# One backbone step on one core: the order of the attention stage and of its weight stream changed

## The chip, the core and the metric

One NeuronCore of a Trainium2 chip runs the whole kernel in one launch. The metric is device time in microseconds (us), median of three runs. All numbers are fp32.

Five engines work side by side, each through its own instructions in order: PE (matmuls; PEld is its weight load), DVE (vector), ACT (activation functions and copies), POOL, and SP, which here does nothing but issue the large weight transfers. They meet through semaphores.

## The reference

Two groups of 128 tokens (context and latent, 256 columns together), width 1024, two layers. Cut to the stage that matters here, layer 0:

```python
h = rmsnorm(x, norm_mix_g[l]) * (1 + sc1) + sh1          # sh1, sc1, g1, sh2, sc2, g2 from silu(cond) @ w_ada[l]
a, q, k, v = split_ab(h @ w_in)                          # 512 pooling, 512 query, 128 key, 128 value columns
y = concatenate([pool_mixer(a, w_pool, pool_scale),      # centred means of 2, 4, 8, 16 tokens, then 4 matmuls
                 attention(q, k, v, sink)], axis=-1)     # 8 heads; latent queries see latent and cached keys
x = x + g1 * (y @ w_out)
h = rmsnorm(x, norm_ffn_g[l]) * (1 + sc2) + sh2
x = x + g2 * hierarchical_moe(h, ...)                    # router, then 16 experts of 3 matrices, 2 per token
```

Layer 1 has a convolution module in the place of pooling and attention, and then its own router and experts. Each layer's six modulation vectors need a 1024 by 6144 matrix `w_ada`.

## The kernel before, in words

**The weight stream.** All large weights come through SP in tiles of 2 MB (the last input tile has 1 MB), 131 of them, in one order, `STREAM`, written by `weight_stream`. `("in", 0, n)` are the three tiles of the input projection: 0 the pooling columns, 1 the queries, 2 keys and values. `("out", 0, n)` are the two of the output projection: 0 the rows that the pooling half multiplies, 1 the rows of the heads' half. `ADA_...` are groups of modulation tiles, each named after the stage in which it is read. `w1`, `w3`, `w2` are the experts' tiles, six for a pair of experts.

**Slots.** A tile lands in one of nine places: six ring slots, and `spare`, `bench` and `back`, which other data occupy until the points named in `joins`. `place_tiles` gives each tile of the stream, in order, the first free slot in the order in which slots become free. Where the slot was used, SP waits until PE has finished the tile that was there (`tiles_used`, a count that PE raises in stream order). SP's queue is strictly in order: a load that waits holds back all behind it, even those whose slot is free.

**PE's order** is the order of the code: transposes and norm, `ADA_SCALE_0` and `ADA_SHIFT_0`, the projections of pooling, queries, keys and values (`project`), two tiles of `ADA_PROJ_0`, the rotation of queries and keys, two more tiles, context and latent scores, `ADA_SOFTMAX_0`, the four tiles of `ADA_ROUTE_0`, 24 transposes of the probabilities, the pooling matmuls, probabilities times values, the output projection (pooling half, then heads), the norm, and the router (`moe`), where the two tiles of `ADA_ROOT[0]` are read. Then eight pairs of experts. `ada_rows` multiplies one modulation tile; at the end of a group ACT copies the sums (`take_part`), `ada_turn` transposes them on PE, and DVE adds the bias (`take_mod`).

**Softmax.** DVE takes one maximum for all heads and both groups, ACT makes 16 exponentials with their sums, DVE divides, PE transposes, and DVE and ACT copy the six transposed banks back in turns.

Of the kernel before, what the change touches and what calls it, by code (L numbers as in the profile page):

```python
# [15 lines left out]
P = 128  # L16
# [6 lines left out]
DC = D // P  # L23
# [80 lines left out]

def weight_stream():
# [13 lines left out]
def place_tiles():  # L119

    joins = {ADA_ROUTE_0[-1]: (BENCH, SPARE), ADA_ROOT[0][-1]: (BACK,),
# [24 lines left out]
def backbone(nc, x_prompt, x_sample, cache_k, cache_v, c, c_ctx, w_ada, b_ada, norm_mix_g, norm_ffn_g,  # L146
# [3 lines left out]
    with ExitStack() as ctx:  # L150
# [8 lines left out]
        ps_part = ps[:, 7, :]  # L159
        ps_ada = ps[:, 6, 384:480].rearrange("p (m g) -> p m g", g=2)  # L160
# [164 lines left out]
        kv_ready = sem("kv_ready")  # L325
        scores_done = sem("scores_done")
# [93 lines left out]
        def product(eng, done, kind, l, k):  # L420


            if k < DC - 2:
                eng.wait_ge(done, k // 2 + 1)
            else:
                used(eng, (kind, l, 1))
# [8 lines left out]
        LAST_IN = ("in", 0, 2)  # L435

# [78 lines left out]
        def _(pe):  # L515
# [3 lines left out]
            def ada_rows(keys, j):  # L519

                landed(pe, keys[j])
                w = wtile(keys[j])
                if j == 0 and ADA[keys[0]]:

                    pe.wait_ge(part_ready, ADA[keys[0]])
                for k in range(FC):
                    for h in range(2):
                        at = 2 * (ADA_MOST - 1 - (j - j % 2 + h))  # L530
                        last = mm(ps_part[32 * k:32 * k + 32, :], csil[:, j % 2 * FC + k, at:at + 32],
                                  w[:, k, h * TW:(h + 1) * TW], j == 0 and h == 0, True)
                last.then_inc(tiles_used, 1)
# [73 lines left out]
            def project(key, out, ready=None):  # L607
                landed(pe, key)
                w = wtile(key)
                for m in range(4):  # L610
# [4 lines left out]
                last.then_inc(tiles_used, 1)  # L615

            project(("in", 0, 0), lambda m: psx[:, m, :], h_ready)
            project(("in", 0, 1), lambda m: psx[:, 4 + m, :])
# [26 lines left out]
            for i in range(4):  # L645
                for r in range(2):
                    lo, hi = 64 * r, 64 * r + 64
                    kv = (2 * i + r) // 4
                    mm(ps[:, r, i * P:(i + 1) * P], qT[lo:hi, i, 0:TG], kT[lo:hi, int(kv != r), 0:TG])
            nc_last = None  # L650
            for i in range(4):
                for keys in range(2):
                    for r in range(2):
# [4 lines left out]
                        nc_last = mm(ps[:, 2 + 2 * r + i // 2, at:at + P], qT[lo:hi, i, TG:NT], k)  # L658
# [7 lines left out]
            for n in range(24):  # L666
                if n % 8 == 0:
                    pe.wait_ge(probs_ready, n // 8 + 1)
                last = nc.tensor.transpose(ps[:, n // 4, (n % 4) * P:(n % 4 + 1) * P], probs[:, n, :], ident)  # L669
                if n % 4 == 3:  # L670
                    last.then_inc(pt_done, 1)
            pe.wait_ge(pt_ready, 6)
            pe.wait_ge(pooled_ready, 1)
            for m in range(4):
                last = mm(psx[:, 4 + m, :], poolw[:, m, :], apad[:, m, :, APAD:APAD + TG])
            last.then_inc(pool_done, 1)
# [15 lines left out]
            ada_turn(ADA_ROUTE_0)  # L692
            for n in range(2):
                key = ("out", 0, n)
                landed(pe, key)
                w = wtile(key)
                if n == 0:
                    pe.wait_ge(pool_mixed, 1)
                for m in range(DC) if n else (4, 5, 6, 7, 0, 1, 2, 3):
                    if n == 0 and m == 0:  # L700
                        pe.wait_ge(heads_mixed, 1)
                    for k in range(FC):
                        last = mm(psx[:, m, :], w[:, k, m * P:(m + 1) * P], mixT[:, FC * n + k, :],
                                  n == 0 and k == 0 and m % 2 == 0, n == 1 and k == FC - 1)
                    if n == 1 and m in (1, 3, 5):
                        last.then_inc(y_done[0], 1)
                    if n == 1 and m == DC - 2:

                        for k in range(DC // 2):
                            norm_sum(1, k)  # L710
                last.then_inc(tiles_used, 1)
# [177 lines left out]
            def crowded(l, i):  # L889

                n = i + l * PAIRS
                with nc.body(f"pe_crowded_{n}", parent=pe_at[n], valid_engines=[mybir.EngineType.PE]):

                    pe.wait_ge(ysel_lo[0], n)
                    pe.wait_ge(ysel_hi[0], n)
                    way = pe.value_load(path[0:1, i:i + 1], min_val=0, max_val=2)
# [26 lines left out]
            def moe(l, n):  # L923

                pe.wait_ge(mod_taken, (4, 8)[l])
                for j in range(len(ADA_ROOT[l])):
                    ada_rows(ADA_ROOT[l], j)

                for k in range(DC):
                    pe.wait_ge(h_ready, DC * n + k + 1)  # L930
                    for g in range(2):
                        last = mm(ps_logit[:, g, 0:20], hT[:, k, g * TG:(g + 1) * TG],
                                  wr[:, l, k, :], k == 0, k == DC - 1)
                last.then_inc(route_done, 1)
                ada_turn(ADA_ROOT[l])

                for g in range(2):
                    for k in range(DC):
                        last = nc.tensor.transpose(ps[:, 2 * g + k // 4, (k % 4) * P:(k % 4 + 1) * P],  # L939
                                                   hT[:, k, g * TG:(g + 1) * TG], ident)  # L940
                        if k % 4 == 3:
                            last.then_inc(htok_done, 1)
                pe.wait_ge(mask_ready, l + 1)
# [4 lines left out]
                mm(ps_rank[:, 2, :], ones[:, :], mask[:, 1, :], False, True).then_inc(rank_done, 1)  # L948
                pe.wait_ge(htok_ready, 4 * l + 4)
# [3 lines left out]
                locate(l, 1, ps[:, 7, NT:NT + 1])  # L953
                gather(0, 0, 1)
                for i in range(PAIRS):
# [117 lines left out]
        def _(act):  # L1073
# [71 lines left out]
            def take_first_parts():  # L1145
# [6 lines left out]
            used(act, ("in", 0, 0))  # L1152
            act.wait_ge(s_fill, 3)
            nc.scalar.activation(apad[:, :, :, APAD:APAD + TG],
                                 psx[:, 0:4, :].rearrange("p c (g t) -> p c g t", g=2), ACT.Copy).then_inc(a_ready, 1)
# [6 lines left out]
            take_part(ADA_PROJ_0)  # L1162

            take_part(ADA_SOFTMAX_0)

            act.wait_ge(nmax_ready, 1)
            for h in range(NH):
                nc.scalar.activation(probs[:, h, :], ps[:, h // 4, (h % 4) * P:(h % 4 + 1) * P], ACT.Exp,
                                     bias=nmax[:, 0, h:h + 1], scale=SCALE,
                                     accum_out=rsum[:, 0, h:h + 1]).then_inc(exp_ready, 1)  # L1170
# [855 lines left out]
```

## Time and profile before

| what | us |
|---|---|
| median of three runs (819.95 to 824.09) | 822.08 |
| span of the profiled execution | 821.7 |
| PE busy in it | 760.8 (93%) |
| DMA: 289.67 MB moved | mean 353 GB/s |

The profile is of one execution, whose span is 0.4 below the median of the runs. Times in rows are us from the span's start. "ring<-in_w_ada" names what a row writes and reads; L517 is the line of the helper `mm`, so nearly every matmul bears it, and its tiles tell them apart: `ring,csil` are modulation tiles, `back,ring` projections, `ring,work` experts. One fp32 matmul shows as two records. "PEclk" is the granted share of TensorE's full clock.

### The profile page before, as it was taken

To read this page: it belongs to the slowest core of one execution; us is meant where nothing else is said; L and a number is where in the kernel's file an instruction comes from. 1 tells how busy PE (TensorE), PEld (TensorE's weight loads), DVE (VectorE), ACT (ScalarE), POOL (GpSimd) and SP (SyncE) were. 2 spreads that over 40 slices of the span, in tenths; PEclk is the share of its full clock that TensorE was granted. 3 is DMA by queue.
4 is the path that set the end of the run, shared out by engine and by line. 5 is a ranking of instruction groups with operands and counts; after the bars stand their busy time and mean duration, and the time that the engine had idled before them with its cause. 6 is when DMAs were issued, how large, how long until landed. Compare 5 with 4: busy or idle time off the path is not lost.

```text
span 821.7 us, 10485 instructions
## 1 busy us (share of the span) xinstructions
PE 760.8 (93%) x4071; PEld 426.7 (52%) x4071; DVE 235.0 (29%) x667; ACT 165.6 (20%) x373; POOL 50.2 (6%) x74
## 2 busy tenths in 40 slices
PE   4699889999999999999799999999998989999796
PEld 4387458754344434443488758683334353333344
DVE  2301331531111111011779931451211112121115
ACT  3210420330100010001502862451010000110012
POOL 5023000010000000000100000001000000001000
PEclk9899999889999999999999999969998999999988
DMA  9997999879999999999995259577999909999941
GB/s 293 400 398 256 412 409 430 345 284 427 424 427 426 426 429 425 426 427 413 398 399 228 108 216 429 194 298 313 430 422 424 392 18 424 428 428 427 419 172 55
DMA packets 42643, 289.67 MB, mean 353 GB/s; under 512 B 4418, under 2 KB 5902, under 8 KB 30291
## 3 DMA queue, kind: packets, MB, share of 16 engines
q1 hardware_dynamic: 36752, 275.78, 81.9%
q0 software_dynamic: 5056, 11.98, 3.9%
q10 hardware_dynamic: 770, 1.06, 0.4%
q8 instruction: 39, 0.64, 0.3%
q14 instruction: 26, 0.21, 0.1%
HBM read 285.63 MB, written 8.52 MB: 358 GB/s over the span
## 4 chain that ended last, share of the span: by engine, by line
PE 75%; DMA 16%; issue 3%; DVE 3%; ACT 1%; SPq 1%; POOL 1%; PEld 0%; DVEq 0%; PEldq 0%; POOLq 0%
PE ps L517 71%; DMA ring<-in_conv_w 4%; DMA back<-in_moe_w 4%; DMA spare<-in_moe_w 3%; DMA ring<-in_w_in_ab 3%; DMA ring<-in_w_ada 3%; DVE work L1747 1%; SPq L463 1%; PE ps L939 1%; PE ps L807 1%; PE ps L741 1%; DVE rstd L1484 0%; PE ps L778 0%; POOL work L1365 0%; PE ps L669 0%
## 5 line engine op out<-in xcount | busy, mean ns | idle before, releaser
L517 PE MATMUL ps<-ring,work 128*64 128x512 f32 x1088 | 304.5, 595 | 3.0 <-issue 2.0
L517 PEld LDWEIGHTS ps<-ring,work 128*64 128x64 f32 x1088 | 94.6, 137 | 144.9 <-issue 144.8
L517 PE MATMUL ps<-back,ring 128*128 128x256 f32 x656 | 148.3, 388 | 6.3 <-DMA ring<-in_conv_w 2.6
L517 PEld LDWEIGHTS ps<-back,ring 128*128 128x128 f32 x656 | 125.7, 194 | 28.1 <-issue 4.2
L517 PE MATMUL ps<-bench,work 128*64 128x512 f32 x208 | 96.1, 611 | 2.0 <-DVE work L1704 1.4
L517 PE MATMUL ps<-spare,work 128*64 128x512 f32 x176 | 80.4, 611 | 4.7 <-issue 4.7
L517 PE MATMUL ps<-back,work 128*64 128x512 f32 x160 | 72.0, 597 | 0.0
L1747 DVE TENSOR_TENSOR work<-work,ps 128x256 f32<-128x256 f32 x34 | 19.4, 611 | 162.9 <-PE ps L517 162.9
L517 PE MATMUL ps<-ring,csil 128*32 128x512 f32 x352 | 44.4, 633 | 8.1 <-DMA ring<-in_w_ada 8.1
L1911 DVE SCALAR_TENSOR_TENSOR work<-work,dw 128x256 f32<-128x256 f32 x120 | 50.8, 479 | 1.0
L1198 ACT ACTIVATE work<-ps 128x512 f32<-128x512 f32 x17 | 10.1, 597 | 200.8 <-PE ps L517 200.8
L517 PEld LDWEIGHTS ps<-bench,work 128*64 128x64 f32 x208 | 27.8, 140 | 29.0 <-issue 28.7
L517 PEld LDWEIGHTS ps<-spare,work 128*64 128x64 f32 x176 | 24.3, 141 | 34.3 <-issue 34.3
L517 PE MATMUL ps<-work 128*128 128x256 f32 x176 | 40.9, 386 | 0.0
L517 PEld LDWEIGHTS ps<-work 128*128 128x128 f32 x176 | 32.6, 190 | 12.9 <-issue 8.9
L1191 ACT ACTIVATE work<-ps 128x512 f32<-128x512 f32 x18 | 10.8, 597 | 121.6 <-PE ps L741 97.0
L1431 POOL DMA_INDIRECT part<-hbuf,row_at x14 | 14.4, 1026 | 298.4 <-PE ps L741 274.6
L517 PE MATMUL ps<-work,xtok 128*128 128x128 f32 x128 | 22.1, 346 | 8.2 <-issue 5.1
L517 PEld LDWEIGHTS ps<-back,work 128*64 128x64 f32 x160 | 20.8, 137 | 16.7 <-issue 16.7
L1769 DVE COPY work<-ps 128x512 f32<-128x512 f32 x11 | 7.6, 691 | 74.3 <-PE ps L517 74.3
L517 PEld LDWEIGHTS ps<-ring,csil 128*32 128x32 f32 x352 | 11.9, 113 | 32.0 <-issue 19.5
L517 PE MATMUL ps<-back,ones 128*128 128x256 f32 x96 | 24.6, 408 | 3.8 <-ACT back L1111 2.2
(238 smaller groups left out, 636.4 us busy)
## 6 DMA issues: line engine op xcount, KB each, us to landing
ring<-in_moe_w SPq DMA_DIRECT2D x63, 2048.0 KB, 19.3
ring<-in_w_ada SPq DMA_DIRECT2D x22, 2048.0 KB, 18.3
bench<-in_moe_w SPq DMA_DIRECT2D x12, 2048.0 KB, 20.5
spare<-in_moe_w SPq DMA_DIRECT2D x11, 2048.0 KB, 20.6
back<-in_moe_w SPq DMA_DIRECT2D x10, 2048.0 KB, 21.8
ring<-in_conv_w SPq DMA_DIRECT2D x6, 2048.0 KB, 24.3
ring<-in_w_in_ab SPq DMA_DIRECT2D x2, 2048.0 KB, 25.0
ring<-in_w_out_ab SPq DMA_DIRECT2D x2, 2048.0 KB, 21.2
```

The source lines that it names most:

```text
L463: sp.dma_start(dst, src.rearrange("(k p) n -> p k n", p=P)).then_inc(slot_full[SLOT[n]], 16)
L517: return nc.tensor.matmul(out, lhsT, rhs, start=start, stop=stop, skip_group_check=True)
L741: last = nc.tensor.transpose(ps[:, 4 + half, (k % 4) * P:(k % 4 + 1) * P], hrows[:, k * P:(k + 1) * P], ident)
L807: last = nc.tensor.transpose(ps[:, 6 + f // 2, (f % 2) * P:(f % 2 + 1) * P], hid[:, f * P:(f + 1) * P], ident)
L939: last = nc.tensor.transpose(ps[:, 2 * g + k // 4, (k % 4) * P:(k % 4 + 1) * P], hT[:, k, g * TG:(g + 1) * TG], ident)
L1191: nc.scalar.activation(hsel[:, 0:4, :], ps[:, 4, :].rearrange("p (k j) -> p k j", k=4), ACT.Copy).then_inc(hsel_lo[which], 1)
L1198: nc.scalar.activation(sil, ps[:, 6, :], ACT.Silu).then_inc(sil_ready[r], 1)
L1431: nc.gpsimd.indirect_dma_start(hrows, None, hbuf[l], IndirectOffsetOnAxis(ap=row_at[:, 0:1], axis=0), bounds_check=NT - 1, oob_is_err=Fals ...
L1747: V.tensor_tensor(hid[:, h * 2 * P:(h + 1) * 2 * P].rearrange("s (f p) -> s f p", f=2), sil.rearrange("s (p f) -> s f p", f=FC)[:, f, :], ...
L1769: V.tensor_copy(ysel[:, 512:1024], ps[:, 5, :]).then_inc(ysel_hi[r], 1)
L1911: V.scalar_tensor_tensor(out=cv[k], in0=upad[:, k, :, t:t + TG], scalar=dw[:, k, t:t + 1], in1=cv[k], op0=ALU.mult, op1=ALU.add).then_inc( ...
```

## The change

The same work is done; its order changes.

- **Stream.** Queries, then keys and values, come first; the pooling tile follows two tiles of `ADA_PROJ_0`. The output tiles come before `ADA_ROUTE_0`, the heads' half first.
- **PE.** Half of the pooling projection stands between the rotation and the latent scores, half after them; then the context scores. Probabilities are transposed in two parts, with modulation work between. The heads' half of the output projection comes first, with the pooling matmuls (now in other PSUM banks) in its middle. The four tiles of `ADA_ROUTE_0` move into the router, one of them in two halves between the router's own matmuls; `ADA_ROOT[0]` moves behind the ranks.
- **ACT and DVE.** Maxima, exponentials and divisions are made for the latent group first, then for the context group. DVE takes over the copy of the pooling columns.
- **Waits.** POOL's first gather of layer 0 waits for the turned `ADA_ROOT[0]`; rounds with a crowded expert wait for the gathered rows.

```diff
-    return (ADA_SCALE_0 + ADA_SHIFT_0 + [("in", 0, n) for n in range(3)] + ADA_PROJ_0 + ADA_SOFTMAX_0
-            + ADA_ROUTE_0 + [("out", 0, n) for n in range(2)] + ADA_ROOT[0] + moe(0)
+    return (ADA_SCALE_0 + ADA_SHIFT_0 + [QUERY_IN, LAST_IN] + ADA_PROJ_0[0:2] + [POOL_IN] + ADA_PROJ_0[2:4]
+            + ADA_SOFTMAX_0 + [HEADS_OUT, POOL_OUT] + ADA_ROUTE_0 + ADA_ROOT[0] + moe(0)
...
-    joins = {ADA_ROUTE_0[-1]: (BENCH, SPARE), ADA_ROOT[0][-1]: (BACK,),
+    joins = {HEADS_OUT: (BENCH, SPARE), ADA_ROOT[0][-1]: (BACK,),
...
-            fit = [f for f in free if expert or f[0] < BENCH]
+            fit = [f for f in free if expert or f[0] < SPARE or f[0] == SPARE and f[1] is not None]
...
-            ada_rows(ADA_PROJ_0, 2)
-            ada_rows(ADA_PROJ_0, 3)
-            ada_turn(ADA_PROJ_0)
-
-            pe.wait_ge(a_ready, 1)
+            landed(pe, POOL_IN)
+            project(POOL_IN, lambda m: psx[:, m, :], range(0, 2))
...
-            nc_last.then_inc(scores_done, 1)
-
-            pe.wait_ge(mod_taken, 3)
-            ada(ADA_SOFTMAX_0)
-            for j in range(len(ADA_ROUTE_0)):
-                ada_rows(ADA_ROUTE_0, j)
...
+            last.then_inc(latent_done, 1)
+            project(POOL_IN, lambda m: psx[:, m, :], range(2, 4))
+            ada_rows(ADA_PROJ_0, 2)
+
+            pe.wait_ge(a_ready, 1)
+            for i in range(4):
...
+            last.then_inc(scores_done, 1)
+            ada_rows(ADA_PROJ_0, 3)
...
+            turn_probs((2, 3, 4, 5), {2: 1, 3: 1, 4: 2, 5: 2})
+            ada_turn(ADA_PROJ_0)
+            ada_rows(ADA_SOFTMAX_0, 0)
+            turn_probs((0, 1), {0: 3, 1: 3})
+            ada_rows(ADA_SOFTMAX_0, 1)
             pe.wait_ge(pt_ready, 6)
...
+            landed(pe, HEADS_OUT)
+            pe.wait_ge(heads_mixed, 1)
+            for m in range(DC):
+                last = output(HEADS_OUT, m, True, False)
+                if m == 3:
+
+                    pe.wait_ge(pooled_ready, 1)
+                    for g in range(4):
+                        mixed = mm(ps_pool[:, g, :], poolw[:, g, :], apad[:, g, :, APAD:APAD + TG])
+                    mixed.then_inc(pool_done, 1)
+            last.then_inc(tiles_used, 1)
+            landed(pe, POOL_OUT)
+            pe.wait_ge(pool_mixed, 1)
+            for m in range(DC):
+                last = output(POOL_OUT, m, False, True)
...
+                if l == 0:
+                    for j in range(len(ADA_ROOT[l])):
+                        ada_rows(ADA_ROOT[l], j)
                 pe.wait_ge(htok_ready, 4 * l + 4)
```

What `place_tiles` makes of it, positions 13 to 27 of the stream (slots 0 to 5 are the ring; "after X" is the tile that PE must have finished first):

| position | before | now |
|---|---|---|
| 13 | `ADA_ROUTE_0[0]`, slot 1 | `HEADS_OUT`, slot 1, after `ADA_PROJ_0[1]` |
| 14 | `ADA_ROUTE_0[1]`, slot 2 | `POOL_OUT`, slot 2, after `POOL_IN` |
| 15 to 18 | `ADA_ROUTE_0[2:4]`, `("out",0,0)`, `("out",0,1)` | `ADA_ROUTE_0` |
| 19 | `ADA_ROOT[0][0]`, slot 1, after `ADA_ROUTE_0[0]` | the same tile, slot 1, after `HEADS_OUT` |
| 20 | `ADA_ROOT[0][1]`, slot 2, after `ADA_ROUTE_0[1]` | the same tile, slot 2, after `POOL_OUT` |
| 21 | first `w1`, slot 3, after `ADA_ROUTE_0[2]` | first `w1`, `bench` |
| 22, 23 | `bench`, `spare` | `spare`, slot 3 after `ADA_ROUTE_0[0]` |
| 25, 26 | after `("out",0,0)`, `("out",0,1)` | after `ADA_ROUTE_0[2]`, `[3]` |

SP's queue before, from the second group of modulation tiles to the first experts (in_w_in_ab are input tiles, in_w_out_ab output tiles, in_moe_w experts):

```order
L463 DMA ring<-in_w_in_ab 128x8x512 x2
L463 DMA ring<-in_w_in_ab 128x8x256 [waits tiles_used]
L463 DMA ring<-in_w_ada 128x4x1024 [waits tiles_used] x10
L463 DMA ring<-in_w_out_ab 128x4x1024 [waits tiles_used] x2
L463 DMA ring<-in_w_ada 128x4x1024 [waits tiles_used] x2
L480 DMA ring<-in_moe_w 128x4096 [waits tiles_used]
L480 DMA bench<-in_moe_w 128x4096 [waits s_out,pv_done]
L480 DMA spare<-in_moe_w 128x4096 [waits pool_done]
L480 DMA ring<-in_moe_w 128x4096 [waits tiles_used] x4
```

The same stretch of SP's queue now:

```order
L467 DMA ring<-in_w_in_ab 128x8x512
L467 DMA ring<-in_w_in_ab 128x8x256
L467 DMA ring<-in_w_ada 128x4x1024 [waits tiles_used] x2
L467 DMA ring<-in_w_in_ab 128x8x512 [waits tiles_used]
L467 DMA ring<-in_w_ada 128x4x1024 [waits tiles_used] x4
L467 DMA ring<-in_w_out_ab 128x4x1024 [waits tiles_used] x2
L467 DMA ring<-in_w_ada 128x4x1024 [waits tiles_used] x6
L484 DMA bench<-in_moe_w 128x4096 [waits s_out,pv_done]
L484 DMA spare<-in_moe_w 128x4096 [waits pool_done]
L484 DMA ring<-in_moe_w 128x4096 [waits tiles_used] x5
```

Four modulation tiles moved from ahead of the output tiles to behind them, so that the two tiles of `ADA_ROOT[0]`, last of the six, and behind them all expert tiles, now wait for PE to be done with the output tiles.

PE before, from the rotation to the output projection (bench,cst is the rotation, bench alone the scores, cst,work the transposes, spare the pooling matmuls, work,bench probabilities times values, cst,part a turn):

```order
L517 MATMUL ps<-bench,cst 128x512
L517 MATMUL ps<-bench,cst 128x128
L517 MATMUL ps<-ring,csil 32x512 x16
L517 MATMUL ps<-cst,part 128x4x2 x4
L517 MATMUL ps<-bench 128x128 x24
L517 MATMUL ps<-ring,csil 32x512 x16
L517 MATMUL ps<-cst,part 128x2x2 x4
L517 MATMUL ps<-ring,csil 32x512 x32
L669 MATMUL ps<-cst,work 128x128 x24
L517 MATMUL ps<-spare 128x256 x4
L517 MATMUL ps<-work,bench 64x128 x24
```

PE now, from behind the rotation to the values:

```order
L521 MATMUL ps<-back,ring 128x256 x16
L521 MATMUL ps<-bench 128x128 x16
L521 MATMUL ps<-back,ring 128x256 x16
L521 MATMUL ps<-ring,csil 32x512 x8
L521 MATMUL ps<-bench 128x128 x8
L521 MATMUL ps<-ring,csil 32x512 x8
L678 MATMUL ps<-cst,work 128x128 x16
L521 MATMUL ps<-cst,part 128x4x2 x4
L521 MATMUL ps<-ring,csil 32x512 x8
L678 MATMUL ps<-cst,work 128x128 x8
L521 MATMUL ps<-ring,csil 32x512 x8
L521 MATMUL ps<-work,bench 64x128 x24
```

The pooling projection (back,ring) now surrounds the latent scores, and the 32 matmuls of the four `ADA_ROUTE_0` tiles are gone from ahead of the transposes.

## Rows read from the trace of the kernel before

**Rows 1.** The page's second part: DMA busy tenths in 40 slices.
```profile
DMA  9997999879999999999995259577999909999941
```

**Rows 2.** By stretch: us, busy of five engines, PEclk, DMA share, GB/s.
```profile
185.00:410.00 225.00, 218.44 (x1044) 93.73 (x1040) 46.43 (x116) 28.16 (x59) 8.62 (x16) 1.00 1.01 423
```

**Rows 3.** PE's timeline: start, us, what, [idle before, releaser].
```profile
410.21 4.20 PE L517 MATMUL ps<-back,ring 128*128 128x256 f32 x12 [2.59 <-DMA ring<-in_conv_w]
```

**Rows 4.** Two transfers of line 480: start, and us to landing.
```profile
L480 SPq DMA_DIRECT2D spare<-in_moe_w x1: 328/328/328, 190.4 to 190.4; - x1
...
DMA to landing us min/median/max: 12.0/12.0/12.0
...
L480 SPq DMA_DIRECT2D spare<-in_moe_w x1: 327/327/327, 354.2 to 354.2; - x1
...
DMA to landing us min/median/max: 28.6/28.6/28.6
```

**Rows 5.** The chain of work that ended last: start, us, what; two pairs of experts.
```profile
191.74 14.25 PE ps L517 x64
...
219.04 14.25 PE ps L517 x64
```

**Rows 6.** The same chain in the attention stage.
```profile
39.62 38.20 PE ps L517 x176
...
77.93 8.55 PE ps L517 x68
...
114.54 35.22 PE ps L517 x200
```

**Rows 7.** PE's timeline in the attention stage.
```profile
87.15 1.06 PE L517 MATMUL ps<-cst,part 128*128 128x8 f32 x8 [0.73 <-ACT part L1143]
...
88.14 2.95 PE L517 MATMUL ps<-bench 64*128 64x128 f32 x48
...
91.02 3.68 PE L517 MATMUL ps<-ring,csil 128*32 128x512 f32 x32
...
110.89 2.97 PE L669 MATMUL ps<-cst,work 128*128 128x128 f32 x24
...
119.24 1.06 PE L517 MATMUL ps<-cst,part 128*128 128x8 f32 x8
```

**Rows 8.** DVE's and ACT's timeline in the softmax.
```profile
91.14 1.22 DVE L1561 TENSOR_REDUCE smax<-ps 128x8 f32<-128x1024 f32 x1 [2.70 <-PE ps L517]
...
96.68 0.37 ACT L1168 ACTIVATE work<-ps,nmax 128x128 f32<-128x128 f32 x1
...
99.44 0.51 ACT L1172 ACTIVATE work<-ps,nmax 128x256 f32<-128x256 f32 x1
...
103.03 0.31 ACT L1178 ACTIVATE esink<-esink 128x16 f32<-128x16 f32 x1
...
105.44 2.18 DVE L1577 TENSOR_SCALAR work<-work,rden 128x256 f32<-128x256 f32 x8
...
111.00 0.60 ACT L1143 ACTIVATE part<-ps 128x512 f32<-128x512 f32 x1 [7.67 <-PE ps L517]
...
119.35 1.02 ACT L1184 ACTIVATE back<-ps 128x1024 f32<-128x1024 f32 x1 [4.86 <-PE ps L517]
```

**Rows 9.** A transfer of line 463 that found the queue empty.
```profile
L463 SPq DMA_DIRECT2D ring<-in_w_ada x1: 368/368/368, 69.2 to 69.2; - x1
...
DMA to landing us min/median/max: 7.8/7.8/7.8
```

**Rows 10.** DMA issues: what, count, KB each, median us to landing.
```profile
hbuf<-xtok POOLq DMA_DIRECT2D x4, 512.0 KB, 7.5
```

**Rows 11.** As Rows 2: three stretches around waits of PE.
```profile
410.00:415.00 5.00, 4.79 (x14) 3.91 (x15) 0.14 (x1) 0.00 (x0) 0.00 (x0) 0.66 1.06 390
...
780.00:785.00 5.00, 3.52 (x10) 1.20 (x12) 0.00 (x0) 0.00 (x0) 0.00 (x0) 0.52 1.02 428
745.00:750.00 5.00, 4.03 (x20) 1.38 (x18) 0.00 (x0) 0.60 (x1) 0.00 (x0) 1.00 1.00 421
```

More of the change, by code:

```diff
@@ L418, in used, with product @@
             eng.wait_ge(tiles_used, TILE[key] + 1)
-        def product(eng, done, kind, l, k):
+        def product(eng, done, last, k):
             if k < DC - 2:
@@ L523, in ada_rows, with ada_half @@
                 landed(pe, keys[j])
-                w = wtile(keys[j])
                 if j == 0 and ADA[keys[0]]:
                     pe.wait_ge(part_ready, ADA[keys[0]])
-                for k in range(FC):
[L529 to L533, printed above, removed]
+                ada_half(keys, j, 0)
+                ada_half(keys, j, 1)
+            def ada_half(keys, j, h):
+                w = wtile(keys[j])
+                at = 2 * (ADA_MOST - 1 - (j - j % 2 + h))
+                for k in range(FC):
+                    last = mm(ps_part[32 * k:32 * k + 32, :], csil[:, j % 2 * FC + k, at:at + 32],
+                              w[:, k, h * TW:(h + 1) * TW], j == 0 and h == 0, True)
+                if h:
+                    last.then_inc(tiles_used, 1)
             def ada_turn(keys):
@@ L604, in _, with project @@
             ada(ADA_SHIFT_0)
-            def project(key, out, ready=None):
-                landed(pe, key)
+            def project(key, out, blocks, ready=None):
                 w = wtile(key)
-                for m in range(4):
+                for m in blocks:
                     for k in range(DC):
@@ L691, in _, with output @@
             last.then_inc(pv_done, 1)
[L692 to L695, printed above, removed]
+            pe.wait_ge(mod_taken, 3)
+            ada_turn(ADA_SOFTMAX_0)
+            def output(key, m, first, last_tile):
                 w = wtile(key)
[L697 to L711, printed above, removed]
+                rows = FC * (key == HEADS_OUT)
+                for k in range(FC):
+                    last = mm(psx[:, m, :], w[:, k, m * P:(m + 1) * P], mixT[:, rows + k, :],
+                              first and k == 0 and m % 2 == 0, last_tile and k == FC - 1)
+                return last
+            landed(pe, HEADS_OUT)
[7 more added lines that the diff above has]
+                    mixed.then_inc(pool_done, 1)
+            last.then_inc(tiles_used, 1)
+            landed(pe, POOL_OUT)
+            pe.wait_ge(pool_mixed, 1)
+            for m in range(DC):
+                last = output(POOL_OUT, m, False, True)
+                if m in (1, 3, 5):
+                    last.then_inc(y_done[0], 1)
+                if m == DC - 2:
+                    for k in range(DC // 2):
+                        norm_sum(1, k)
+            last.then_inc(tiles_used, 1)
             norm_sums(1, DC // 2)
@@ L925, in moe @@
                 pe.wait_ge(mod_taken, (4, 8)[l])
-                for j in range(len(ADA_ROOT[l])):
-                    ada_rows(ADA_ROOT[l], j)
+                if l == 0:
+                    ada_rows(ADA_ROUTE_0, 0)
+                    ada_rows(ADA_ROUTE_0, 1)
+                    landed(pe, ADA_ROUTE_0[2])
+                else:
+                    for j in range(len(ADA_ROOT[l])):
+                        ada_rows(ADA_ROOT[l], j)
                 for k in range(DC):
@@ L933, in moe @@
                                   wr[:, l, k, :], k == 0, k == DC - 1)
+                    if l == 0 and k in (2, 4):
+                        ada_half(ADA_ROUTE_0, 2, k // 4)
                 last.then_inc(route_done, 1)
-                ada_turn(ADA_ROOT[l])
+                if l == 0:
+                    ada_rows(ADA_ROUTE_0, 3)
+                else:
+                    ada_turn(ADA_ROOT[l])
                 for g in range(2):
@@ L948, in moe @@
                 mm(ps_rank[:, 2, :], ones[:, :], mask[:, 1, :], False, True).then_inc(rank_done, 1)
+                if l == 0:
+                    for j in range(len(ADA_ROOT[l])):
+                        ada_rows(ADA_ROOT[l], j)
                 pe.wait_ge(htok_ready, 4 * l + 4)
@@ L1185, in _ @@
             norm_act(1, (0, 24))
-            take_part(ADA_ROOT[0])
+            take_part(ADA_ROUTE_0)
             def take_low(which, count):
@@ new lines, in divisor, with divide_latent @@
+            def divisor(g):
+                dve.wait_ge(exp_ready, (NH + 1) * (2 - g))
+                link(V.tensor_tensor(rden[:, g, :], rsum[:, g, :], esink[:, g, :], ALU.add))
+                link(V.reciprocal(rden[:, g, :], rden[:, g, :]))
+            def divide_latent(first):
+                for h in range(first, first + NH // 2):
+                    last = V.tensor_scalar(probs[:, 8 + 2 * h:10 + 2 * h, :], probs[:, 8 + 2 * h:10 + 2 * h, :],
+                                           rden[:, 1, h:h + 1], None, ALU.mult)
+                last.then_inc(probs_ready, 1)
@@ L1573, in _ @@
+            divisor(1)
+            divide_latent(0)
+            dve.wait_ge(scores_done, 1)
+            bound(0, ps[:, 0:2, :], 4)
+            divide_latent(NH // 2)
+            take_turned(2, 1)
+            take_turned(4, 3)
+            divisor(0)
             for h in range(NH):
```

128 lines of the change are left out of this document (66 added, 62 removed).

## The prediction, made before the changed kernel ran

> **What bounds the kernel now.** The page gives PE 93% of the span, so I looked for the stretches in which something else sets the time. First the slices of the DMA engines [rows 1], 20.5 us each: full from the tenth to the twenty-first, 185 to 431 us, and with gaps before, in the fourth (61 to 82), the eighth and the ninth (144 to 185). Then the busy time by stretch [rows 2]: from 185 to 410 the DMA engines are never idle (share 1.01 at 423 GB/s), while PE is busy 218 of 225 us. Then PE's own waits: at 410.2, at the start of layer 1's convolution, it has waited 2.59 us for a convolution tile [rows 3]. So two things end nearly together at 410, PE's work and the weight stream, and the stream is 2.6 us later.
>
> The stream's pace and PE's differ. Position 32 of the stream is issued at 190.4 and lands 12.0 later, at 202.4; position 68, the last expert tile of layer 0, is issued at 354.2 and lands 28.6 later, at 382.8 [rows 4]. The 36 tiles between take 180.4 us, 5.01 each, which is 30.1 for the six tiles of a pair of experts, gathers included. PE needs 219.04 - 191.74 = 27.3 for a pair [rows 5]. PE can therefore live on a lead for a while, but the layer ends when the stream does. After 410 I take the rest as rigid: a shift of the convolution's start shifts the end by as much, since from there PE's chain is followed to the next stretch in which the stream waits for slots that PE sets free.
>
> The question is thus not how early PE leaves the attention stage, but when the stream starts to run without gaps. Before, that is about 185.
>
> **PE in the attention stage.** Per step, what PE has to do from 39.6 to the end of the output projection: projections 38.3 (from 39.62 to 77.93); four tiles of ADA_PROJ_0 with the rotation 8.55 [rows 6]; the turn 1.06, scores 2.95, two tiles of ADA_SOFTMAX_0 3.68, transposes 2.97 [rows 7]; the second turn about 1.06, as the first; then 35.22 for the pooling matmuls, values and output projection [rows 6], less the turn of ADA_ROUTE_0, which goes away from here (119.24 to 120.15, 0.9): 34.3. The sum is 92.9, so PE could be done at 132.5. The four tiles of ADA_ROUTE_0 (two cost 3.68 [rows 7], so 7.4) and the waits for their transfers go from here.
>
> What waits come in their place? I follow PE through the new order with the same rows. Queries and keys end at 63.4, two modulation tiles and the rotation at 68.3, half of the pooling projection (7.2 of its 14.5) at 75.6, latent scores at 77.5, the other half at 84.7, a modulation tile at 86.6, context scores at 87.5, another tile at 89.4. DVE's copy of the pooling columns is hidden: they are ready at 84.7, the maximum over as many columns costs 1.22 [rows 8], PE needs the banks at 86.6; without that cover it would cost those 1.2. The latent exponentials begin after 80 and are eight of 0.45, done before 85. Three waits stay:
> - The second half of the latent division. DVE takes four divisions (half of 2.18), the context maximum (1.22 and about 0.4 for its small steps), then four more [rows 8]: ready at 90.6, PE there at 90.4: 0.3.
> - The turn of ADA_PROJ_0. On ACT the copy of its sums now stands behind the context exponentials: maximum ready at 89.2, eight exponentials in 2.76 (96.68 to 99.44), the sink 0.31, the copy 0.60 [rows 8], so 93.0; PE has done 16 transposes and stands since 91.6: 1.4.
> - The copy of the heads' output, 1.02 on ACT [rows 8], less the turn of ADA_SOFTMAX_0 that PE does meanwhile: 0.3.
>
> That is 2.0, and the output projection ends at 134.5, against 149.8 before: 15.3 earlier. The pooling chain on POOL, the pooling matmuls and the probabilities' last copies are done before PE asks for them.
>
> **The router.** It gets 7.4 us of tiles and a turn, partly in waits that were there. Even if all 8.4 came on top, PE would reach the experts 6.9 earlier than before. That is not where the end is set.
>
> **The stream.** SP issues in order. Position 14 now waits for the pooling tile (84.7), position 19 for the heads' half of the output projection (about 118.7), position 20 for its end (134.5); the experts' tiles stand behind, those for bench and spare too, though these are free by 113. Before, positions 13 to 20 needed modulation and input tiles alone, which PE had done by 104, and the stream ran without a gap from 82 to 144.
>
> A modulation tile that found the queue empty landed 7.8 after its issue [rows 9]. So position 20 lands at 134.5 + 7.8 = 142.3, and from there nothing holds the stream: positions 23 to 27 need the tiles of ADA_ROUTE_0 and ADA_ROOT[0] done, which PE has by about 156, before the stream comes to them. Twelve tiles at 5.01 are 60.1. The two stores of the token rows (hbuf, 512 KB each [rows 10]), which fell into a gap before, now share the engines: at 423 GB/s [rows 2] 2.5 us; bounds are 0, if they fall beside other gaps, and twice as much; I take 2.5. Position 32 lands at 142.3 + 60.1 + 2.5 = 204.9, against 202.4: the stream is 2.5 us later, and stays so, since it is full from there to 410 either way. PE, 7 or more earlier, uses up its lead against the slower stream in three pairs (2.8 a pair) and then waits for tiles. The last pair's w2 waited for its tile before too, so the end of the layer moves with the stream.
>
> The sum: 821.7 + 2.5 = 824.2 for a profiled execution. The median of the runs stood 0.4 above the profiled one, so 824.5. Bounds from the unknowns: no new waits of PE (-2.0) and hidden stores (-2.5) give 820.0; a later end of the output projection counts one for one.
>
> The landing time is where the notes differ. The Trainium skill, "DMA: Bandwidth & Descriptors", section "Anatomy of one DMA", puts a transfer at 2.0 us and its bytes at 436 GB/s (fitted on GpSimd's path, while these are SP's), an estimate of 6.8 for a 2 MB tile; the row has 7.8. By the page the sum would be 823.5; I keep the row.
>
> **Rivals.**
> *The new chain through ACT and DVE is longer than its rows (slower).* ACT now holds 16 exponentials, two sinks and the copy of ADA_PROJ_0 in one line, DVE three divisions, two maxima and the pooling copy. If each step of it costs its semaphore hops and the context group comes 4 us later, PE stands at the turn of ADA_PROJ_0, the output projection ends at 138.5, and the end is 828.5. It decides from an end later than 136. For it: five hand-overs between DVE and ACT that are one now. Against it: the rows already hold such hops, and PE has modulation tiles to put between.
>
> *The clock (slower).* Starved pairs wait 2.8 us, mostly in one place, between w1 and w3. After the wait of 2.59 at 410 the granted clock was 0.66 over five us; around the longer wait of 780 it was 0.52, the lower of the two levels (1.2 of 2.4 GHz); around a wait of under 1 us at 746 it was 1.00 [rows 11]. If every starved pair falls to the lower level for some 5 us, it loses about 2.5, nearly the 2.8 it had; what is left over at the last pair, at most 2.5, is half covered by the 2.59 that PE waits at 410: end 825 to 827, say 826.5. The Trainium skill, "TensorE: Matmul & The Clock Gate", section "HAM oscillation", tells of a kernel that waits for DMA before each group of matmuls and starts each of them cold; by that rule all five starved pairs would fall.
>
> *PE sets the end after all (faster).* If the stream has slack that I don't see, for example because the gaps before cost it more than those now, PE's lead counts. The convolution could start at 410.2 - 2.6 - 6.9 = 400.7, and the end be 812.5. For it: PE's share, and no wait of PE from 185 to 380. Against it: the DMA share of 1.01 over the whole stretch.
>
> **How the numbers follow.** The forecast has 0.60, the longer chain 0.17, the clock 0.13, PE's lead 0.10. A difference under 0.5% (4.1 us) can't be told from none with runs that spread from 819.95 to 824.09. The forecast itself, 820 to 828, is 0.52 within that bound and 0.08 above; the chain is 0.14 above and 0.03 within; the clock 0.05 and 0.08; PE's lead 0.09 below and 0.01 within. Together: faster 0.09, same 0.64, slower 0.27. The range, 819.5 to 830, leaves out PE's lead and the worst of the chain; the forecast's own is 820 to 828.
>
> **What would show it.** Right: the output projection ends at 133 to 137; between 83 and 143 the DMA engines have three gaps, the last two about ten us each; from 143 to the convolution they are full; from the fourth pair on PE waits for experts' tiles; the convolution starts near 413. Wrong: gaps that are missing because the loads don't wait as I read them, a convolution that starts before 408 (then the stream was not the bound), or an attention stage that ends after 137.

## The result, and the profile of the changed kernel

| | before | changed |
|---|---|---|
| median of 4 runs each, us | 821.02 (818.44 to 824.09) | 837.77 (836.36 to 837.92) |
| ratio, with its 95% interval | | 1.0192 (1.0169 to 1.0215) |
| profiled execution, us; its span | 822.08; 821.7 | 836.36; 834.6 |

The changed kernel is 1.9% slower. The forecast was 824.5, with 819.5 to 830 as its range: wrong in size, and the time lies outside it. The page's DMA slices first, 20.9 us each here, against [rows 1]:

```profile
DMA  9999753999999999999998159577999908999951
```

The engines are full from the eighth slice to the twenty-first, and the gaps before now stand in the fifth to seventh, 83 to 146. Busy time by stretch shows the last two (columns as in [rows 2]), then the saturated stretch:

```profile
117.00:130.00 13.00, 13.00 (x62) 11.42 (x62) 1.66 (x4) 0.00 (x0) 0.00 (x0) 1.00 0.11 21
135.00:146.00 11.00, 10.71 (x49) 8.71 (x47) 3.38 (x12) 2.50 (x6) 0.00 (x0) 1.00 0.13 23
185.00:423.00 238.00, 225.10 (x1061) 98.57 (x1058) 44.08 (x110) 28.14 (x60) 8.94 (x17) 0.99 1.01 423
```

SP's transfers of positions 20, 32 and 68, which answer to [rows 4, 9]:

```profile
L467 SPq DMA_DIRECT2D ring<-in_w_ada x1: 368/368/368, 143.8 to 143.8; - x1
...
DMA to landing us min/median/max: 8.0/8.0/8.0
...
L484 SPq DMA_DIRECT2D ring<-in_moe_w x1: 328/328/328, 196.2 to 196.2; - x1
...
DMA to landing us min/median/max: 19.5/19.5/19.5
...
L484 SPq DMA_DIRECT2D ring<-in_moe_w x1: 328/328/328, 364.8 to 364.8; - x1
...
DMA to landing us min/median/max: 32.6/32.6/32.6
```

Position 20 is issued at 143.8, when the output projection's last tile has been used, and lands at 151.8. Position 32 lands at 196.2 + 19.5 = 215.7, against 202.4 [rows 4], and position 68 at 397.4, against 382.8. The stream is 13 to 15 late, and the span grew by 12.9.

So the gate works as forecast, but this last gate, the issue of position 20, opens at 143.8 instead of 134.5. Where the 9.3 went is in the chain of work that ended last, in the attention stage (start, us, what; to be held against [rows 6]):

```profile
65.46 20.86 PE ps L521 x132
86.32 0.02 issue
86.34 1.23 DVE spare L1636
...
87.91 5.17 DVE work L1622 x4
93.09 1.14 DVE smax L1606
...
95.68 2.61 DVE work L1622 x4
...
98.34 1.97 PE ps L678 x8
```

L1622 is the division of the latent probabilities. In [rows 8] eight of them took 2.18; here the first four take 5.17 and the next four 2.68 (2.61 in the chain). The same line by itself (ns of one, shortest/median/longest), and POOL's timeline at that time:

```profile
L1622 DVE TENSOR_SCALAR work<-work,rden x8: 340/878/1983, 87.9 to 97.4; 128x256 f32<-128x256 f32 x8
```
```profile
87.66 2.09 POOL L1442 TENSOR_TENSOR spare<-spare 128x1144 f32<-128x1144 f32 x1 [75.51 <-DVE spare L1636]
89.83 0.64 POOL L1447 TENSOR_TENSOR mean<-spare,cst 128x256 f32<-128x256 f32 x1
90.54 0.72 POOL L1450 TENSOR_TENSOR spare<-mean,spare 128x256 f32<-128x256 f32 x1
91.34 1.60 POOL L1442 TENSOR_TENSOR spare<-spare 128x846 f32<-128x846 f32 x1
```

The longest division, 1.98, lies beside POOL's longest sum, 2.09. The first four take 1.98, 0.79, 0.88 and 1.75, and each of them ends 0.1 to 0.2 after one of these four instructions of POOL (2.09, 0.64, 0.72 and 1.60): each of these divisions waits out one whole instruction of POOL. The pooling columns now come so late that POOL's chain runs from 87.7 to 99.7, beside DVE's divisions. PE stands behind them, and what follows the second wait is slow as well (PE's timeline, then the stretch with its granted clock, 0.56 of full):

```profile
93.14 1.09 PE L678 MATMUL ps<-cst,work 128*128 128x128 f32 x8 [2.04 <-DVE work L1622]
98.34 1.97 PE L678 MATMUL ps<-cst,work 128*128 128x128 f32 x8 [4.10 <-DVE work L1622]
100.10 1.72 PE L521 MATMUL ps<-cst,part 128*128 128x8 f32 x8
101.74 3.64 PE L521 MATMUL ps<-ring,csil 128*32 128x512 f32 x16
105.32 1.26 PE L678 MATMUL ps<-cst,work 128*128 128x128 f32 x8
```
```profile
97.00:107.00 10.00, 8.66 (x48) 5.19 (x52) 5.29 (x16) 2.67 (x9) 2.51 (x4) 0.56 0.73 272
```

The theory to be tested: DVE's divisions are slowed by POOL's pooling chain; the clock adds a part of its own; and the end follows the moment at which the output projection's tiles are free, since the experts' tiles stand behind two loads that wait for them. Rivals: something else slows the divisions, or PE's own late start at the experts sets the end.

### The profile page after: what moved, and what is told of

It reads as the page before. It is cut to its first block, busy times and chain, and to the rows that moved or that the text cites. A ratio compares the mean times of both kernels' runs of the same rounds, so it can differ in the third digit from the quotient of the medians.

```text
span 834.6 us, 10496 instructions
## 1 busy us (share of the span) xinstructions
PE 766.7 (92%) x4071; PEld 426.7 (51%) x4071; DVE 243.6 (29%) x673; ACT 164.5 (20%) x373; POOL 50.4 (6%) x74
## 3 DMA queue, kind: packets, MB, share of 16 engines
q10 hardware_dynamic: 770, 1.06, 0.4%
## 4 chain that ended last, share of the span: by engine, by line
PE 71%; DMA 17%; DVE 4%; issue 4%; ACT 1%; POOL 1%; PEld 1%; DVEq 0%; SPq 0%; PEldq 0%; POOLq 0%
PE ps L521 68%; DMA back<-in_moe_w 8%; DMA ring<-in_moe_w 4%; DMA hbuf<-xtok 2%; DMA ring<-in_w_ada 2%; DMA part<-hbuf,row_at 1%; DVE work L1813 1%; DVE work L1622 1%; PE ps L831 1%; PE ps L975 1%; DVE rstd L1530 1%; PEld ps L521 1%; PE ps L765 1%; PE ps L678 0%; POOL work L1409 0%
## 5 line engine op out<-in xcount | busy, mean ns | idle before, releaser
L521 PE MATMUL ps<-ring,work 128*64 128x512 f32 x1088 | 321.6, 598 | 12.4 <-issue 11.7
L521 PEld LDWEIGHTS ps<-ring,work 128*64 128x64 f32 x1088 | 100.6, 137 | 160.2 <-issue 160.0
L521 PE MATMUL ps<-back,ring 128*128 128x256 f32 x592 | 134.5, 387 | 3.5 <-ACT back L1177 3.1
L521 PEld LDWEIGHTS ps<-back,ring 128*128 128x128 f32 x592 | 113.5, 194 | 22.5 <-issue 5.7
L521 PE MATMUL ps<-bench,work 128*64 128x512 f32 x208 | 97.9, 620 | 3.5 <-DVEq L1526 2.0
L521 PE MATMUL ps<-ring,csil 128*32 128x512 f32 x368 | 52.0, 701 | 2.9 <-DMA ring<-in_w_ada 2.9
L521 PEld LDWEIGHTS ps<-work 128*128 128x128 f32 x176 | 32.5, 190 | 12.9 <-issue 8.9
L521 PE MATMUL ps<-back,ones 128*128 128x256 f32 x96 | 22.9, 386 | 3.8 <-ACT back L1156 2.2
```

Of the source, the lines that this page charges most:

```text
L521: return nc.tensor.matmul(out, lhsT, rhs, start=start, stop=stop, skip_group_check=True)
```

## The experiments

**The pooling chain later.** On POOL, in the changed kernel:

```diff
             pool.wait_ge(a_ready, 1)
+            pool.wait_ge(probs_ready, 3)
             src, at = apad, 0
```

> The changed kernel, with one more wait: POOL starts the pooling chain only when DVE has finished all divisions of the probabilities. Theory (DVE's divisions run slowly because POOL's pooling chain runs at the same time): the eight divisions of 128x256 take 0.27 us each, as before the change, instead of 1.29 and 0.67; PE's two waits for them, 2.04 and 4.10, shrink to about 0.3 and 1.4, the clock does not fall to 0.50 behind them; the output projection ends near 136 instead of 143.8, and the time falls by 7 to 8, to about 830. Rival A (the divisions are slow because of ACT, the PE or the transfers, not POOL): they stay at 5.17 and 2.68 for four, and the time stays at 837.8. Rival B (the end of the output projection is not what sets the time): the divisions are fast, the stage ends near 136, and the time stays above 834.

Measured: 829.09 (827.59 to 830.50, 6 runs) against 822.02 (22 runs); ratio 1.0088 (1.0057 to 1.0119). DVE's timeline, then PE's:

```profile
89.26 1.14 DVE L1623 TENSOR_SCALAR work<-work,rden 128x256 f32<-128x256 f32 x4
...
92.40 1.14 DVE L1623 TENSOR_SCALAR work<-work,rden 128x256 f32<-128x256 f32 x4
```
```profile
92.39 2.30 PE L678 MATMUL ps<-cst,work 128*128 128x128 f32 x16
95.86 1.06 PE L521 MATMUL ps<-cst,part 128*128 128x8 f32 x8 [1.18 <-ACT part L1188]
96.85 3.14 PE L521 MATMUL ps<-ring,csil 128*32 128x512 f32 x16
99.92 1.51 PE L678 MATMUL ps<-cst,work 128*128 128x128 f32 x8
```

The divisions are as fast as before, PE's two waits are gone, and the wait of 1.4 that the prediction had put at the turn appears there, with 1.18. Position 20 is issued at 138.6. That is 2.6 later than expected. Half of it is the start: this execution came to the modulation tiles and the rotation at 66.7, the changed kernel at 65.4. The other half is the clock, which I had expected to stay up (0.74 granted from 95 to 100): behind the wait of 1.18 the next tile took 3.14 instead of 1.92 and the transposes behind it 1.51 instead of 1.09. Both rivals fall: half of the loss is gone by a wait on POOL alone.

**The same collision, made in the kernel before.** There the pooling chain ran before the scores:

```diff
             pool.wait_ge(a_ready, 1)
+            pool.wait_ge(exp_ready, 17)
             src, at = apad, 0
```

> The kernel before, with one more wait: POOL starts the pooling chain only when ACT has finished the exponentials, so that it runs beside DVE's divisions (in the kernel before it ran at 56 to 69, when DVE was idle). Theory (POOL's chain slows DVE's divisions): the eight divisions of 128x256 take 5 to 10 us together instead of 2.18, and the eight of 128x128 more than 1.66 too. Rival (something else in the new order slows them): 2.18 and 1.66 as they were. The time is expected within 3 of the kernel before in either case, since there the stream does not wait for this stage; it is not the question of this run.

Measured: 828.91 in one run, span 827.1. DVE's timeline in the kernel before and here, then POOL's here:

```profile
103.86 1.66 DVE L1574 TENSOR_SCALAR work<-work,rden 128x128 f32<-128x128 f32 x8
```
```profile
104.91 5.36 DVE L1575 TENSOR_SCALAR work<-work,rden 128x128 f32<-128x128 f32 x8
110.19 6.75 DVE L1578 TENSOR_SCALAR work<-work,rden 128x256 f32<-128x256 f32 x8
```
```profile
104.54 2.09 POOL L1399 TENSOR_TENSOR spare<-spare 128x1144 f32<-128x1144 f32 x1 [92.40 <-ACT esink L1178]
```

6.75 instead of 2.18 [rows 8], and 5.36 instead of 1.66 for the eight of the context group, without any other part of the change: the cause is POOL. My expectation for the time missed. The span rose by 5.4, since in the kernel before a stream tile waits for the output projection as well: position 26, issued at 149.8 before and here at 156.2 (1.0 of it a later start of the stage), and position 32 lands 6.5 later, at 208.9.

**Two experts' tiles ahead of the two that wait.** SP alone, in the changed kernel:

```diff
-            for key in STREAM[:TILE["w1", 0, 0]]:
+            for key in STREAM[:TILE[ADA_ROOT[0][0]]]:
                 load(key)
...
                         expert_tile(i, t, 2 * i + t % 2)
+                        if l == 0 and i == 0 and t == 1:
+                            for key in ADA_ROOT[0]:
+                                load(key)
```

> The changed kernel, with one edit on SP alone: the first two experts' tiles, whose places are free when the heads' values and the pooling matmuls are done, are issued ahead of the two tiles of ADA_ROOT[0], which wait for the output projection's two tiles. PE's order is the same. Theory (the stream behind those two waits sets the time): the two experts' tiles are issued near 111 and 121 and fill the idle time of the DMA engines; the output projection still ends near 143.8; position 32 of the stream lands 10 earlier, near 206; the convolution starts near 413, and the time falls by about 10, to 828. Rival (PE's own late start at the experts, 178.1 instead of 175.0, sets the time): the tiles come earlier, PE does not, and the time stays above 834.

Measured: 826.33 (823.66 to 829.85, 11 runs) against 822.02; ratio 1.0055 (1.0033 to 1.0078). SP's timeline, then the stretch that had a DMA share of 0.11:

```profile
110.18 0.34 SPq L484 DMA_DIRECT2D bench<-in_moe_w  x1
120.26 0.34 SPq L484 DMA_DIRECT2D spare<-in_moe_w  x1
```
```profile
117.00:130.00 13.00, 13.00 (x62) 11.42 (x62) 1.66 (x4) 0.00 (x0) 0.00 (x0) 1.00 0.86 323
```

The divisions are as slow as in the changed kernel and the last gate opens at 142.7, but position 32 lands at 193.6 + 11.6 = 205.2, ten earlier, and the time falls by 11. PE begins the experts at 176.8, only 1.3 earlier. It is the stream that sets the end, and PE's start does not.

**Both edits.** The wait on POOL and the order on SP, as above.

> Both edits: the late pooling chain, and the two experts' tiles ahead of ADA_ROOT[0]. Theory: the two gains are of different kinds and add up as far as the stream goes, 7.5 + 10: position 32 near 198, experts on PE from about 171; then PE and the stream are again nearly level, and the time is 820 to 822, level with the kernel before. Rival (behind the faster stage PE's own work or the late gather of the second pair sets the time): 825 or more, with PE never waiting for a tile of the stream between 200 and 400.

Measured: 821.34 (818.17 to 824.19, 12 runs) against 822.02; ratio 0.9991 (0.9969 to 1.0014). Alone the two edits gained 8.7 and 11.4, together they gain 16.4 of these 20. Position 32 lands at 200.3 (198 was expected), and PE and the stream are nearly level, as in [rows 3]. The wait at the turn is as long as with the first edit alone, but here the clock stayed up: the tile behind it takes 1.92, not 3.14 (PE's timeline):

```profile
94.81 1.06 PE L524 MATMUL ps<-cst,part 128*128 128x8 f32 x8 [1.17 <-ACT part L1191]
95.80 1.92 PE L524 MATMUL ps<-ring,csil 128*32 128x512 f32 x16
...
408.14 3.72 PE L524 MATMUL ps<-back,ring 128*128 128x256 f32 x16 [1.98 <-DMA ring<-in_conv_w]
```

**The latent divisions on ACT.** POOL stays beside them:

```diff
+            act.wait_ge(rden_ready, 1)
+            for h in range(NH):
+                last = nc.scalar.activation(probs[:, 8 + 2 * h:10 + 2 * h, :], probs[:, 8 + 2 * h:10 + 2 * h, :],
+                                            ACT.Copy, scale=rden[:, 1, h:h + 1])
+                if h % 4 == 3:
+                    last.then_inc(probs_ready, 1)
...
-            divide_latent(0)
+            dve.sem_inc(rden_ready, 1)
...
-            divide_latent(NH // 2)
```

> The changed kernel, with the eight divisions of the latent probabilities on ACT in place of DVE; POOL's pooling chain stays where it is, beside them. Theory (only DVE is slowed by POOL): ACT's divisions take about 0.4 each whatever POOL does, 1.6 for four, and PE's two waits of 2.04 and 4.10 go; DVE's eight context divisions of 128x128 now fall beside the end of POOL's chain and take 3 to 5 instead of 1.66, which costs PE a new wait of 1 to 3 ahead of the last eight transposes. Output projection near 138.5, time near 832. Rival (whatever works on the probabilities beside POOL is slowed): ACT's divisions take over 0.8 each, and the time stays above 836.

Measured: 830.59 (828.61 to 835.89, 4 runs) against 822.77 (17 runs); ratio 1.0117 (1.0076 to 1.0157). ACT's timeline, then DVE's:

```profile
86.39 3.30 ACT L1216 ACTIVATE work<-work,rden 128x256 f32<-128x256 f32 x8 [2.13 <-DVEq L1646]
```
```profile
87.72 1.22 DVE L1613 TENSOR_REDUCE smax<-ps 128x8 f32<-128x1024 f32 x1 [1.42 <-PE ps L522]
...
89.96 1.45 DVE L1618 TENSOR_TENSOR esink<-nmax,sink 128x8 f32<-128x8 f32 x1
...
94.39 3.39 DVE L1653 TENSOR_SCALAR work<-work,rden 128x128 f32<-128x128 f32 x8
```

Beside POOL, ACT takes 3.30 for eight; in the next run, with POOL idle then, it takes 3.30 too. DVE's maximum, which reads PSUM, keeps its 1.22 [rows 8], while an addition of 128x8 out of SBUF takes 1.45, and the context divisions 3.39 instead of 1.66. So it is DVE's work on SBUF that POOL holds up; ACT, on the same probabilities, is not held up. The new wait of PE ahead of the last transposes did not come: the clock was at 0.50 from 95 to 100, and PE was late itself.

**All three edits.** The wait on POOL, the order on SP, the divisions on ACT.

> Three edits: the late pooling chain, the two experts' tiles ahead of ADA_ROOT[0], and the latent divisions on ACT. With the first two alone the run took 821.3 against 822.0 before. Theory: DVE's 2.2 of divisions leave the chain to the context maximum, PE's last wait of 1.17 in the transposes goes, the output projection ends at 134 to 135 instead of 135.9, and the time is 819 to 821. Rival (PE's waits were gone already, and ACT's divisions delay its context exponentials by 3): output projection at 137 to 138, time 822 to 824.

Measured: 819.00 (814.77 to 822.60, 12 runs) against 822.77; ratio 0.9960 (0.9939 to 0.9981). This version beats both kernels, by 0.4% the one before. But the theory missed. PE's last wait did not go, it grew from 1.17 to 1.67 (below), and from the start of the rotation's step to the last gate it took 72.0, against 70.2 with two edits. The last gate opened at 135.3 instead of 135.9 only because this execution came to that step at 63.3 instead of 65.7. The medians, 2.3 apart, come from two series of runs, and their intervals against the kernel before overlap. That the third edit adds something is therefore not shown, and its own stage speaks against it. PE still waits at the convolution, for less:

```profile
92.55 1.32 PE L525 MATMUL ps<-cst,part 128*128 128x8 f32 x8 [1.67 <-ACT part L1192]
...
407.42 3.72 PE L525 MATMUL ps<-back,ring 128*128 128x256 f32 x16 [1.03 <-DMA ring<-in_conv_w]
```

**The waits filled.** Useless matmuls in PE's two waits keep the engine at work (`{2: 8, 4: 16}` first, then half):

```diff
                 for b in banks:
+                    for _ in range({2: 4, 4: 8}.get(b, 0)):
+                        mm(ps[:, 6, 0:NT], rot, kT[:, 0, :])
                     pe.wait_ge(probs_ready, taken[b])
```

> The changed kernel, with matmuls of no use (rotation matrix times keys, 128x256, results never read) in PE's two waits for the divisions: 8 in the first, 16 in the second, 0.23 us each, so that PE works through them. The divisions stay slow. Theory (part of the loss is the clock: it fell to 0.50 behind the wait of 4.10, and the next four steps took 1.97, 1.72, 3.64 and 1.26): the granted clock stays near 1.00, these steps take 1.09, 1.06, 1.92 and 1.09, the output projection ends 3.4 earlier, near 140.4, and the time is near 834.5. Rival (the clock falls for another reason, or what is won is waited for at the next step): the output projection ends within 1 of 143.8, time 837 to 838.

> As the run with filled waits, but with half as many useless matmuls, 4 and 8. There 16 and 32 passes were recorded (3.72 and 7.07 us), longer than the waits they were to fill, so that the output projection ended 78.9 after the start of the rotation, no earlier than the 78.4 of the changed kernel, though the clock stayed at 1.00. With half, 1.9 and 3.5 us fit into the waits of 2.04 and 4.10. Theory (the clock is a part of the loss of its own): the granted clock stays at 1.00, transposes, turn, tile and transposes take 1.09, 1.06, 1.92 and 1.09, and the output projection ends 75 after the rotation's start, so 3.4 less; against the longer filling it also shows whether an end 4 later costs 4. The time is 833 to 835. Rival (the fall of the clock costs the end nothing): 78 again, and 837 to 838.

Measured: with 8 and 16, 833.19 (829.20 to 835.64, 4 runs) against 822.77, ratio 1.0121 (1.0087 to 1.0154); with 4 and 8, 830.01 (828.24 to 832.72, 8 runs) against 822.60 (13 runs), ratio 1.0080 (1.0043 to 1.0116). PE's timeline of the second, and its stretch at that time:

```profile
92.86 3.62 PE L521 MATMUL ps<-bench,cst 128*128 128x256 f32 x16
97.14 1.09 PE L680 MATMUL ps<-cst,work 128*128 128x128 f32 x8 [0.66 <-DVE work L1624]
98.08 0.96 PE L521 MATMUL ps<-cst,part 128*128 128x8 f32 x8
98.96 1.92 PE L521 MATMUL ps<-ring,csil 128*32 128x512 f32 x16
```
```profile
95.00:100.00 5.00, 4.34 (x35) 3.17 (x38) 4.78 (x13) 3.09 (x13) 3.24 (x5) 1.00 1.03 410
```

With the divisions as slow as ever, the four steps run at the full clock and the gate opens 74.9 after the rotation, 3.5 less than in the changed kernel. So the clock is a part of the loss of its own, and the rival falls. The first filling was too long and gave the 3.5 back, as its 78.9 shows; its gate opened 3.4 later than the second's, and its span is 4.8 longer, 833.8 against 829.0. The time of the second is 3 under what I expected, of which 1.2 are an earlier start of the stage in the profiled execution. The rest of it is not explained, nor that the first one's median lies 2.5 under its own profiled execution (835.64).

## Why the prediction was wrong

| run | rotation starts | last gate opens | between | position 32 lands | span |
|---|---|---|---|---|---|
| forecast | 63.4 | 134.5 | 71.1 | 204.9 | 824.2 |
| changed | 65.4 | 143.8 | 78.4 | 215.7 | 834.6 |
| POOL later | 66.7 | 138.6 | 71.9 | 210.7 | 828.7 |
| divisions on ACT | 63.8 | 137.8 | 74.0 | 209.9 | 829.2 |
| waits overfilled | 63.6 | 142.5 | 78.9 | 215.0 | 833.8 |
| waits filled | 64.2 | 139.1 | 74.9 | 210.8 | 829.0 |

The rotation is counted, here as above, with the two modulation tiles ahead of it. In all ten profiled executions, those of the kernel before and of the other stream orders too, the span ends 617.6 to 619.3 after position 32 has landed, while the landing lies anywhere from 199.7 to 215.7. This is the plainest sign that the stream sets the end.

**What held.** The bound (the weight stream), the three positions that gate it, their order on SP, the landing after 8, the twelve tiles behind. From the last landing to position 32 it is 63.9, against 62.6 forecast. The five profiled executions with the changed stream order follow the gate: with POOL later it is 5.2 earlier, and the span 5.9 shorter. With the gate at 134.5, one for one, the five rows give a span of 824.4 to 825.9, where I had 824.2.

**The step that failed** is "four divisions (half of 2.18)" in "The second half of the latent division", and so the three waits of "2.0" and "the output projection ends at 134.5". An attention stage that ends after 137 was among the signs of being wrong that the prediction named. The duration was read from a row in which DVE had SBUF to itself, and it was carried into a place where POOL's chain, 12 us long, had been moved as well. I wrote of that chain only that it is done before PE asks for it, and did not ask what it does to others meanwhile. By rows, the 9.3 are: 6.1 of waits at the divisions, where waits of 0.3 and 1.4 had been forecast there and at the turn, 4.4; the clock on four steps, 1.97 + 1.72 + 3.64 + 1.26 against 1.09 + 1.06 + 1.92 + 1.09, 3.4; a start 2.0 later; that is 9.8, half a microsecond over. With POOL out of the way the same stage took 71.9 and, with both edits, 70.2, against 71.1 forecast, so the rest of its working stands.

The Trainium skill has the rule that I left out: "SBUF — State Buffer", section "Who interferes with whom", gives DVE and GpSimd one pair of SBUF ports between them, taken as a lock for a whole instruction; a `tensor_scalar` of DVE can enter a mode that needs the pair, a `tensor_reduce` never does on this chip, and ACT waits for nobody. The runs agree as far as they go: 1.98 beside 2.09, and 1.75 beside 1.60; 1.22 unchanged, though of a maximum that reads PSUM; 3.30 with POOL and without. They show that whole instructions of POOL hold DVE up; that a pair of ports is the reason, no run here shows.

**The later start** differs between profiled executions: the rotation starts at 63.3 to 66.7 in eight kernels whose work up to there is the same, with granted clocks of 0.50 to 0.75 between 30 and 35. That stretch alone does not order them, since the earliest and the latest both have 0.50 there, and the four of the later series start at 63.3 to 64.2, those ahead of them at 64.3 to 66.7. What sets the start is not shown.

**The rivals.** The longer chain through ACT and DVE came nearest: slower, in the right place, and by its own test ("It decides from an end later than 136"). Its mechanism, hand-overs between the engines, was not it. The clock cost something, though not in starved pairs of experts (0.99 granted from 185 to 423) but behind the waits of this stage. PE's lead decided nothing. PE came to the experts 3.1 later than before, and still it waited for tiles in the pairs, first in the sixth, at 326.69 (the chain stands on an experts' transfer there, from 305.8 to 335.6), and not, as I wrote, from the fourth on (PE's timeline; "issue" is what the trace names where it sees no releaser):

```profile
178.14 1.09 PE L521 MATMUL ps<-bench,work 128*64 128x512 f32 x1 [2.03 <-DVEq L1526]
...
326.69 7.09 PE L521 MATMUL ps<-ring,work 128*64 128x512 f32 x32 [1.34 <-issue]
```

The router took 34.4 from the last gate to the experts; in the run with POOL later, with more of the full clock there, 29.6.

**The rest of the gap**, 837.8 to 824.5: the span explains 10.4. Of the other 2.9, 1.4 lie between the profiled execution and the median, and 1.4 in a measured time that stood 1.8 above the span, where in the row before it was 0.4. That 0.4, which the forecast carried over, was the odd one: in the 52 later executions of the kernel before the time stands 1.7 to 1.9 above the span as well.

**Sums that do not come out.** The parts that the prediction names add up to 0.61 for the same time and 0.30 for slower, where it writes 0.64 and 0.27; and 824.2 with 0.4 is 824.6, not 824.5. Neither changes the argument.

## What to carry to other kernels

When a change moves work in time, ask of each moved instruction not only whether it is ready when wanted, but what now runs beside it: a duration holds only next to the neighbours that it was measured with, and for DVE on SBUF the neighbour is POOL. Where a weight stream sets the end, look on the queue for loads that wait behind the critical stage and put those ahead whose places are free; here that gave 11 us without touching PE. A stage that is freed of waits can gain twice, since PE's clock may stay up: filling the waits gave 3.5 here with the divisions as slow as ever.

## What the runs showed of the hardware

- A DVE division of 128x256 in SBUF takes 0.34 alone and 0.73 to 1.27 beside POOL's pooling chain in the kernel before, up to 1.98 in the changed one; even an addition of 128x8 rose from 0.17 to 1.45. There each of the first four waited out one whole instruction of POOL. POOL's own instructions barely noticed: the first sum took 2.09 in all these runs, and the others rose by up to 0.07.
- Behind the wait of 4.10 the granted clock was 0.56 over ten us; with the divisions on ACT it was 0.50 from 95 to 100 behind a wait of only 2.08 (the lower of the two levels, 1.2 of 2.4 GHz). Behind waits of 1.18 and 1.17 at the same step it fell once (a tile of 3.14) and once it did not (1.92), so the length of that wait alone does not decide it.
- The store of the token rows took 17.5 from issue to landing beside a saturated stream (165.6 to 183.2 in the chain); the median of the four such stores was 7.5 before [rows 10] and 12.1 after. PE waited 2.08 for the gather behind it, in the second pair.
